# Moving the round trip of the kernel rows of a state-space stage from SP's DMA queue to ACT's

## The reference

```python
bu_re = jnp.einsum('bsgc,gpc->bsgp', u, bb_re)
bu_im = jnp.einsum('bsgc,gpc->bsgp', u, bb_im)
...
_, _, xr, xi = lax.associative_scan(combine, (a_re, a_im, bu_re, bu_im), reverse=reverse, axis=1)
return (jnp.einsum('bsgp,gcp->bsgc', xr, c_re.astype(f32))
        - jnp.einsum('bsgp,gcp->bsgc', xi, c_im.astype(f32)))
...
y = (s5_direction(ug, ..., False) + s5_direction(ug, ..., True)
     + d_skip.astype(f32).reshape(B_GROUPS, B_GROUP) * ug)
```

## Time and profile before

| | us |
|---|---|
| median of 3 runs | 2278.11 |
| lowest, highest | 2278.03, 2278.43 |
| time of the profiled execution | 2278.34 |
| its span in the trace | 2276.6 |

### The profile page before, as it was taken

The page is one execution under the profiler, slowest core; times in us unless marked ns, Lnnn a source line. Parts: engine busy times, 40 slices in busy tenths (PEclk is TensorE's granted clock), DMA queues, the critical chain, the costliest instruction groups (busy, mean ns, idle before and its releaser), DMA issues.

```text
span 2276.6 us, 40505 instructions
## 1 busy us (share of the span) xinstructions
PE 2225.2 (98%) x14035; PEld 1961.4 (86%) x14035; DVE 1551.7 (68%) x2541; ACT 1018.9 (45%) x1465; POOL 166.2 (7%) x154
## 2 busy tenths in 40 slices
PE   6998979999999999999999999999999999999997
PEld 6997868888888888888888888888888888888886
DVE  7799367676576566567677777767756756766765
ACT  7620266544444444444454545444444444444442
POOL 1000002300000000000420000131000000000032
PEclk9999999999999999999999999999999999999999
DMA  8546555667657557567666565666666566566563
GB/s 229 167 124 153 139 185 157 189 190 206 188 185 210 189 187 210 187 191 202 187 196 186 176 189 170 185 186 186 192 185 184 191 196 189 189 192 187 184 194 111
DMA packets 438952, 418.00 MB, mean 184 GB/s; under 512 B 49627, under 2 KB 434859, under 8 KB 438348
## 3 DMA queue, kind: packets, MB, share of 16 engines
q1 hardware_dynamic: 435952, 414.30, 60.1%
q10 hardware_dynamic: 2908, 2.51, 0.4%
HBM read 406.35 MB, written 10.39 MB: 183 GB/s over the span
## 4 chain that ended last, share of the span: by engine, by line
PE 91%; DVE 6%; DMA 1%; ACT 1%; issue 0%; SPq 0%; DVEq 0%; ACTq 0%
PE psum L1579 54%; PE psum L1580 28%; PE psum L1576 2%; PE psum L1553 2%; DVE ysum L934 2%; PE psum L1755 1%; DVE whl L934 1%; DVE fa L934 1%; DVE wv L934 1%; DMA raw<-in_ab_w_in 1%; PE psum L1737 0%; DMA bias_a<-t_rel 0%; PE psum L1806 0%; PE psum L1732 0%; PE psum L1775 0%
## 5 line engine op out<-in xcount | busy, mean ns | idle before, releaser
L934 DVE TENSOR_TENSOR whl<-raw,whl 128x1024 fp32r<-128x1024 f32 x712 | 878.0, 1244 | 486.2 <-ACT whl L560 484.4
L560 ACT ACTIVATE whl<-raw 128x1024 fp32r<-128x1024 f32 x712 | 754.9, 1061 | 754.4 <-PE psum L1580 682.6
L1579 PE MATMUL psum<-act,whl 128*128 128x512 f32 x2560 | 892.5, 394 | 0.0
L1580 PE MATMUL psum<-act,whl 128*128 128x256 f32 x2560 | 713.6, 279 | 0.0
L1579 PE MATMUL psum<-hid,whl 128*128 128x512 f32 x2048 | 710.3, 392 | 0.0
L1579 PEld LDWEIGHTS psum<-act,whl 128*128 128x128 f32 x2560 | 479.7, 187 | 109.4
L1580 PE MATMUL psum<-hid,whl 128*128 128x256 f32 x2048 | 570.4, 279 | 0.0
L1580 PEld LDWEIGHTS psum<-act,whl 128*128 128x128 f32 x2560 | 482.3, 188 | 0.1
L1579 PEld LDWEIGHTS psum<-hid,whl 128*128 128x128 f32 x2048 | 383.5, 187 | 86.7
L1580 PEld LDWEIGHTS psum<-hid,whl 128*128 128x128 f32 x2048 | 385.7, 188 | 0.0
L571 ACT ACTIVATE half<-psum 128x256 f32<-128x256 f32 x344 | 113.7, 382 | 286.8 <-PE psum L1580 286.0
(11 more groups left out here) (201 smaller groups left out, 1789.9 us busy)
## 6 DMA issues: line engine op xcount, KB each, us to landing
raw<-in_mlp_w SPq DMA_DIRECT2D x512, 512.0 KB, 4.0
raw<-in_c_w_qkv SPq DMA_DIRECT2D x96, 512.0 KB, 4.6
raw<-in_ab_w_in SPq DMA_DIRECT2D x64, 512.0 KB, 4.2
raw<-in_ab_w_out SPq DMA_DIRECT2D x32, 512.0 KB, 4.4
raw<-in_c_w_out SPq DMA_DIRECT2D x32, 512.0 KB, 4.4
raw<-in_s_w_glu SPq DMA_DIRECT2D x8, 512.0 KB, 3.6
bias_c<-rpb_pad SPq DMA_DIRECT2D x64, 64.0 KB, 2.5
rpb_pad<-rpbw SPq DMA_DIRECT2D x4, 889.0 KB, 10.6
```

What stands on the lines that cost most here:

```text
L560: nc.scalar.activation(whl[:, s, :, 0, :], raw[:, s], ACT.Copy).then_inc(hi_done, 1)
L934: return nc.vector.tensor_tensor(dst, s0, s1, op)
L1579: pe.matmul(bank, *big, start=first, stop=False, skip_group_check=True)
L1580: last = pe.matmul(bank[:, 0:T], *little, start=False, stop=final, skip_group_check=True)
```

## The change

`store_k` and `load_m` are moved, word for word, from SP's program into ACT's. On ACT, `store_k` stands in the loop over blocks behind `take_tiles(10)`, and `load_m` behind `take_tiles(11)`. Semaphores, sizes and access patterns are the same; the line numbers of what lies between shift by 21 or less.

```diff
@@ SP's program
-            def store_k():
-                sp.wait_ge(k_ev, 4)
-                sp.wait_ge(k_mid, 6)
-                for q in range(4):
...
-            def load_m():
-                sp.wait_ge(k_out, 16 * 4)
-                for g in range(2):
-                    for j in range(LC):
...
-                if n == 45:
-                    store_k()
-                if n == 47:
-                    load_m()
@@ ACT's program
+            def store_k():
+                a.wait_ge(k_ev, 4)
+                a.wait_ge(k_mid, 6)
+                for q in range(4):
+                    dst = bass.AP(tensor=k_dram.tensor, offset=q * CH * LAGS * CH,
+                                  ap=[[LAGS * CH, CH], [4 * CH * LAGS * CH, NG // 4], [1, LAGS * CH]])
+                    a.dma_start(dst, kst[32 * q:32 * q + CH].rearrange("p g m c -> p g (m c)")).then_inc(k_out, 16)
+
+            def load_m():
+                a.wait_ge(k_out, 16 * 4)
+                for g in range(2):
+                    for j in range(LC):
...
+                        a.dma_start(mloc[r:r + CH].rearrange("p q j c -> p q (j c)"), src).then_inc(m_in, 16)
...
                 after(j, 3)
+                if j == 10:
+                    store_k()
+                if j == 11:
+                    load_m()
```

More of the change, by code:

```diff
@@ L360, in load_u @@
                         sp.dma_start(u2[r:r + CH, QP * jb:QP * (jb + 1), g, :], src).then_inc(u_in[jb], 16)
-            def store_k():
-                sp.wait_ge(k_ev, 4)
-                sp.wait_ge(k_mid, 6)
-                for q in range(4):
-                    dst = bass.AP(tensor=k_dram.tensor, offset=q * CH * LAGS * CH,
-                                  ap=[[LAGS * CH, CH], [4 * CH * LAGS * CH, NG // 4], [1, LAGS * CH]])
-                    sp.dma_start(dst, kst[32 * q:32 * q + CH].rearrange("p g m c -> p g (m c)")).then_inc(k_out, 16)
-            def load_m():
-                sp.wait_ge(k_out, 16 * 4)
-                for g in range(2):
-                    for j in range(LC):
[L374 to L377, removed]
             def store_y(r):
@@ L688, in take_kernel @@
                 nc.scalar.activation(dst[:, :, LC:LAGS], fwd[:, :, 1:LC], ACT.Copy).then_inc(k_ev, 1)
+            def store_k():
[9 more added lines that the diff above has]
+                    for j in range(LC):
+                        src = bass.AP(tensor=k_dram.tensor, offset=g * CH * LAGS * CH + (LC - 1 - j) * CH,
+                                      ap=[[LAGS * CH, CH], [2 * CH * LAGS * CH, NPAIR], [1, LC * CH]])
+                        r = NST * g + CH * j
+                        a.dma_start(mloc[r:r + CH].rearrange("p q j c -> p q (j c)"), src).then_inc(m_in, 16)
             def take_round(r):
```

## The result

| | before | after |
|---|---|---|
| median us, 20 runs each | 2277.73 | 2281.03 |
| lowest, highest | 2275.57, 2282.32 | 2279.83, 2282.60 |
| span of the profiled execution | 2276.6 | 2278.4 |

The ratio of after to before is 1.0014, with a 95% interval of 1.0008 to 1.0021. The change costs 3.3 us. That is less than the 0.2% of the prediction, but clear of noise over 20 runs. The forecast was 2278.3 us and its range ended at 2280.4 us.

A forecast was written before the change was run, and what follows sets the result against it. PE was taken as the bound, its gaps caused by SP's queue, then by DVE's scan. 2278.34 - 1.44 (earlier start) + 1.6 (low clock) = 2278.5 us, forecast as 2278.3 against the median; range 2276.5 to 2280.4 us.

The forecast's parts named there:

- the 0.2% of the prediction: Smallest difference from no change that a measurement of this kernel can tell, 4.56 us; no change had chance 0.93.
- Part 1: Weight loads on SP's queue: subs 46 to 49 load on time, PE reaches round 0 at 227.8 instead of 236.29 us.
- Part 2: Before round 0: DVE's scan is late next, so only 1.44 us of 8.6 arrives and PE has a 7.1 us gap.
- Parts 4 and 5: ACT's added waits and issues, and `mloc` reads beside weight loads on two queues: each was to cost 0.
- The 3 us of room that I gave the weights: Weight loads beside the `mloc` reads: issued 10.5 us before need, landing in 7.3 us, so 3 us left.
- the second term of the sum: PE at round 0: the +1.6 us added for running at the low clock behind the new gap.
- Part 3: PE's clock behind the new gap: round 0 begins at 1.2 GHz, costing 1.6 us, between 0 and 1.9.
- The bound of 1.9 us: PE behind the new gap: upper limit for the price of one stretch at the half clock.
- the third rival: Round 0: its small 64-row products do not raise the fallen clock; +5.8 us, 2283.9 us, chance 0.04.
- The prediction's own list of signs: Profile signs around round 0 that would show the forecast right or wrong, such as one gap of some 7 us.
- one more short stretch in the heads: Heads behind round 0: another stretch at the half clock, +1.6 us, setting the range's upper end at 2280.4 us.
- the forecast's own range: Whole kernel: 2277.7 to 2278.8 us, with 1.2 to 1.9 us for the low clock; chance 0.80.

The follow-up runs named there:

- e3: Kernel before with only `load_m` moved to ACT's queue, the stores staying on SP: 2276.68 us, ratio 0.9995.
- e7: Changed kernel with 17 extra products of unused result filling PE's gap before round 0: 2278.14 us, ratio 0.9995.
- e8: Kernel before with `store_k` and `load_m` still on SP's queue but later, behind the loads of subs 48 and 50: 2281.36 us, ratio 1.0013.
- e2: Changed kernel with sub 53 between the wait for the scan and round 0, each later sub ahead of the next round: 2280.93 us, ratio 1.0010.
- e6: Kernel before, rows on SP's queue, with subs 53 and 54 ahead of round 0, sub 55 between rounds 1 and 2: 2282.55 us, ratio 1.0020.
- e0: Changed kernel executed once more, nothing altered: 2279.36 us in a single execution.
- e10: Changed kernel with 8 extra products behind sub 52, leaving a gap of 4.12 us before round 0: 2282.38 us, ratio 1.0017.
- e4: Kernel before with only `store_k` moved to ACT's queue, the reads staying on SP: 2279.39 us, ratio 1.0006.
- e5: Changed kernel with subs 53 and 54 ahead of round 0, sub 55 between rounds 1 and 2: 2275.14 us, ratio 0.9984.

## Why the prediction was wrong

**What held.** SP's queue and its fault of 8.6 us (Part 1): PE is through sub 52 without a wait for `raw`. What is late next (Part 2): the scan, a gap of 7.45 us where 7.1 were forecast, and a start 1.42 us earlier; the traces of e3 and e7 show that gain alone. The cost on ACT and of two queues (Parts 4 and 5) was nothing that the medians or the traces show, as e8 and e7 say from both sides, though not with the sizes I gave: beside the reads a load of weights took 8.7 us and a read of `mloc` up to 10.1 us to land, by these rows of the changed kernel's DMA view, 203 to 220 us, and of its view of `mloc`:

```profile
raw<-in_ab_w_in SPq DMA_DIRECT2D x5, 512.0 KB, 8.7
...
mloc<-k_rows ACTq DMA_DIRECT2D x8, 128.0 KB, 7.4
```

```profile
DMA to landing us min/median/max: 5.5/7.4/10.1
```

The 3 us of room that I gave the weights was 1.8.

**The step that failed is the second term of the sum, in Part 3.** I took 1.6 us for the low clock; it cost 5.4 us, 3.13 in round 0 and 2.23 in the sub behind it. The bound of 1.9 us was no bound. I had taken it from two gaps, both with products on all 128 rows and columns behind them, and the length of a low stretch was taken over with the price. Even for large products it does not hold: 3.0 us in e2, 3.1 us in e6. The place of the new gap is another: round 0 has only small products, on 64 rows or columns, and they did not raise the clock. I had this as the third rival, at 2283.9 us, and gave it 0.04, on the ground that PE is dense in the round. PE is: 8.40 of 8.40 us busy, and the clock stays down. The forecast should have weighed what stands behind the gap, not how busy PE is there. The rival's own price, +5.8 us, was too high: the round does not double at the half clock, it goes from 5.3 to 8.4 us. The prediction's own list of signs had it: it is wrong "if the clock stays at 0.50 through round 0".

With 5.4 in the place of 1.6 the sum is 2278.1 - 1.4 + 5.4 = 2282.1 us; measured 2281.0. The trace has 3.94 us up to round 3 and the medians 3.3. The other executions with the low clock in round 0 have 3.56 (e0), 2.54 (e8) and 3.95 us (e10), so single executions differ by more than the 0.6 us that is left over; where it goes is open.

The rule of the Trainium skill that I weighed ("TensorE: Matmul & The Clock Gate", section "HAM oscillation") held in direction: the burst behind the wait pays, 5.4 us here. How much it pays I took from my rows, and these had large products behind their gaps.

The range's upper end came from one more short stretch in the heads and not from this rival, and so missed the median by 0.6 us. At its lower end the forecast's own range took 1.2 us as the least price of the clock, where Part 3 had 0 and no row has 1.2. The chances by the 0.2% bound were right in that the change is within it.

## What to carry to other kernels

A stall that is removed ahead of a fixed later event only moves to that event. Before removing it, look at what stands behind the new place of the gap: if that is small products like those of round 0, the low clock can last through all of it, and the moved gap is then dearer than the stall was. Move whole, large, independent products into the gap together with the change: here the moved queue alone cost 3.3 us, and with three subs moved as well the gain was 6.8.

## What the hardware showed that I had not expected

- The low clock outlives full activity. 8.4 us of products on 64 rows or columns, with PE busy all the time, left it at 0.50 in four executions (the change, its repeat, e8, e10); it rose 1.7 to 4.6 us into sub 53. Large products right behind a gap raised it within the first sub: after 6 us in e2 and in e6, after 3 us in e4. What makes the difference (the part of the array in use, the length of a product, the share of weight loads) the runs do not separate.
- The same products, entered at 1.00, keep it there: for 5.3 us in each round of the kernel before, and for 10.6 us on end in e5. Raising the clock and keeping it are not the same.
- A gap of 4.12 us before round 0 had the same price as one of 7.45 us, and one of 1.59 us had none. In between, 2.88 us had none before a large sub, and 3.05 us before the heads had one (e5).
- At half the clock round 0 took 1.6 times as long (8.4 against 5.3 us), not twice.
